# An attention stage of one 128-token tile, with and without an identity matmul per item whose result nobody reads

## The reference

```python
def one_block(args):
    q_i, k_i, v_i, m_i = args
    s_loc = jnp.where(m_i, jnp.einsum('bqkgd,bskd->bkgqs', q_i, k_i).astype(jnp.float32), NEG_INF)
    s_ctx = jnp.einsum('bqkgd,blkd->bkgql', q_i, k_ctx).astype(jnp.float32)
    p = jax.nn.softmax(jnp.concatenate([s_loc, s_ctx, sink_col], axis=-1), axis=-1).astype(v.dtype)
    return (jnp.einsum('bkgqs,bskd->bqkgd', p[..., :n_loc], v_i)
            + jnp.einsum('bkgql,blkd->bqkgd', p[..., n_loc:n_loc + L], v_ctx))
```

## Time and profile before

| | |
|---|---|
| median of three runs | 3007.74 us (3006.69 to 3013.98) |
| the profiled execution's own time | 3018.25 us |
| its span, first to last instruction | 3015.9 us |
| mean granted clock of TensorE over the span | 0.815 of full speed |
| PE busy | 2077.2 us, 69% of the span |
| DVE busy | 1703.2 us, 56% |
| POOL busy | 1703.4 us, 56% |

### The profile page before, as it was taken

How to read it: one execution, slowest core, us unless ns; L and a number is a source line. 1 busy time by engine, 2 the same in 40 slices (tenths; PEclk the granted TensorE clock), 3 DMA queues, 4 the chain that set the end, 5 groups by cost and what they waited for, 6 DMA issues and landing times.

```text
span 3015.9 us, 23744 instructions
## 1 busy us (share of the span) xinstructions
PE 2077.2 (69%) x7806; PEld 908.8 (30%) x7806; DVE 1703.2 (56%) x4169; ACT 371.9 (12%) x753; POOL 1703.4 (56%) x1541
## 2 busy tenths in 40 slices
PE   6998857778886885566566565567968766555555
PEld 2445542224542541111112111113755333111111
DVE  1224496657876686454545664523479677566551
ACT  1111111002211110010011100101212111000000
POOL 0000035766666767777876776760025776777775
PEclk9997978888888897887787776688885998667789
DMA  6462377999899999999999999994167999999998
GB/s 196 156 199 77 98 244 282 406 392 377 320 344 364 359 374 391 399 398 398 398 402 355 349 379 346 367 342 149 40 225 240 370 384 391 372 369 391 388 409 309
DMA packets 339769, 961.00 MB, mean 319 GB/s; under 512 B 27952, under 2 KB 112064, under 8 KB 339264
## 3 DMA queue, kind: packets, MB, share of 16 engines
q0 software_dynamic: 221184, 805.40, 70.4%
q1 hardware_dynamic: 114448, 146.60, 14.3%
q10 hardware_dynamic: 4016, 7.49, 0.7%
HBM read 958.33 MB, written 1.05 MB: 318 GB/s over the span
## 4 chain that ended last, share of the span: by engine, by line
POOL 31%; PE 28%; DMA 15%; DVE 13%; issue 12%; ACT 1%; SPq 0%; POOLq 0%; ACTq 0%; DVEq 0%
POOL v_rows L401 16%; POOL u_rows L401 15%; DMA v_rows<-in_peer_v,idx_turned 12%; PE ps L504 7%; PE ps L704 6%; PE ps L439 3%; DVE u_rows L1341 3%; PE ps L635 2%; PE ps L673 2%; PE ps L429 1%; PE ps L575 1%; DMA u_rows<-in_peer_u,idx 1%; PE ps L466 1%; PE ps L554 1%; PE ps L553 1%
## 5 line engine op out<-in xcount | busy, mean ns | idle before, releaser
L704 PE MATMUL ps<-v_rows,spread_w 128*32 128x512 f32 x3072 | 958.9, 778 | 743.1 <-DMA v_rows<-in_peer_v,idx_turned 714.3
L401 POOL DMA_INDIRECT u_rows<-in_peer_u,idx x768 | 857.2, 1116 | 982.4 <-DVE idx L1284 556.7
L1341 DVE CUSTOM_DVE_ANT_0 u_rows<-u_rows,h 128x1024 f32<-128x1024 f32 x768 | 924.5, 1223 | 570.2 <-DMA u_rows<-in_peer_u,idx 567.7
L401 POOL DMA_INDIRECT v_rows<-in_peer_v,idx_turned x768 | 844.2, 1099 | 315.5 <-issue 221.1
L704 PEld LDWEIGHTS ps<-v_rows,spread_w 128*32 128x32 f32 x3072 | 193.9, 127 | 1369.7 <-issue 1331.8
L504 PE MATMUL ps<-wring,arena 128*128 128x512 f32 x576 | 268.5, 623 | 9.3 <-DVE arena L1002 7.2
L439 PE MATMUL ps<-wring,silu_c 128*2 128x256 f32 x768 | 203.1, 426 | 10.2 <-DMA wring<-in_mod_w 10.2
L673 PE MATMUL ps<-arena,wring 128*128 128x256 f32 (+1 forms) x1024 | 190.6, 342 | 2.8 <-ACT h L870 2.8
L673 PEld LDWEIGHTS ps<-arena,wring 128*128 128x128 f32 x1024 | 163.0, 201 | 47.6 <-issue 28.7
L504 PEld LDWEIGHTS ps<-wring,arena 128*128 128x128 f32 x576 | 113.6, 202 | 163.8 <-issue 150.5
L429 PE MATMUL ps<-table,arena 128*128 128x128 f32 (+1 forms) x480 | 89.9, 317 | 51.6 <-ACT arena L753 32.9
(11 more groups left out here) (159 smaller groups left out, 1737.0 us busy)
## 6 DMA issues: line engine op xcount, KB each, us to landing
wring<-in_mod_w SPq DMA_DIRECT2D x48, 1024.0 KB, 15.7
wring<-in_peer_w_q SPq DMA_DIRECT2D x32, 1024.0 KB, 9.6
wring<-in_ab_w_in SPq DMA_DIRECT2D x28, 1024.0 KB, 5.3
wring<-in_swa_w_in SPq DMA_DIRECT2D x14, 1024.0 KB, 10.8
u_rows<-in_peer_u,idx POOLq DMA_INDIRECT x768, 6.6
v_rows<-in_peer_v,idx_turned POOLq DMA_INDIRECT x768, 6.6
wring<-in_ab_w_out SPq DMA_DIRECT2D x8, 1024.0 KB, 6.4
wring<-in_swa_w_out SPq DMA_DIRECT2D x8, 1024.0 KB, 7.4
```

The source lines that it names most:

```text
L401: nc.gpsimd.indirect_dma_start(out=ring[:, n, :], out_offset=None, in_=table, in_offset=bass.IndirectOffsetOnAxis(ap=index, axis=0)).then_ ...
L704: mm = nc.tensor.matmul(PS[32 * q:32 * q + 32, 6 + e, :], spread_w[:, s // PAIR % 2, 32 * c:32 * c + 32], VB[:, x % NV, e * 512:(e + 1) * ...
L1341: nc.vector.tensor_tensor_reduce(UB[:, slot % NU, :], UB[:, slot % NU, :], H2[:, g // 8 % 3, :], 1.0, 0.0, ALU.mult, ALU.add, av_[:, 0, g ...
```

## The change

`keep_busy` and its call are taken out. Nothing else differs, on any engine; all 18 matmuls of it go, and no semaphore, wait or buffer changes.

```diff
@@ -515,12 +515,6 @@
                         mm.then_inc(pr_tr, 1)
                     yield
 
-            def keep_busy(p):
-
-
-                if p == 2:
-                    nc.tensor.matmul(PS[:, 6, 0:TOK], ident, TB[:, T_MASK:T_MASK + TOK], start=True, stop=True)
-
             def attn(p):
                 i0, i1 = I_OF[p]
                 j = [0, 1, 4, 4][p]
@@ -554,7 +548,6 @@
                             nc.tensor.matmul(PS[:, i % 2, 0:TOK], q, k[:, 0:TOK], start=False, stop=True)
                             mm = nc.tensor.matmul(PS[:, i % 2, TOK:2 * TOK], q, k[:, TOK:2 * TOK], start=True, stop=True)
                         mm.then_inc(at_s, 1)
-                    keep_busy(p)
                     if i0 <= i - 1 < i1:
                         m = i - 1
                         pe.wait_ge(at_exp, m + 1)
```

## The result

The changed kernel takes 3033.87 us (median of 7 runs, 3026.69 to 3039.25); the kernel before, in the runs beside it, 3007.74 us (3000.13 to 3019.04, 7 runs). The ratio is 1.0074, with a 95% interval of 1.0043 to 1.0104. The profiled execution of the changed kernel took 3031.06 us, its span is 3029.3 us. Of all executions behind this document one was slow, one of the ten of fill_keep (7280.29 us), and it is not counted.

What follows compares the result with a forecast made beforehand. PE alone was taken to bound the pass 2 attention; staying at 1.2 GHz gave +17.2 us to L466 and +2.0 in `outp(2)`, together +19.2: 3037.4 from the profiled time, 3026.9 from the median. It took 3034, range 3011 to 3043.

Steps and rivals of the forecast that it cites:

- PE is the bound, without and with L522: Pass 2 attention: PE alone holds the path at both clocks; 1.9 us of slack at full clock, 1.35 without L522.
- The clock stays low through pass 2: Pass 2 attention without L522 stays at 1.2 GHz throughout, items 5.61 us as in pass 3; forecast case 67%.
- The removal of 18 L522: Pass 2 items: each identity matmul removed saves 1.01 us at low clock, 0.54 at full; six ran low, twelve full.
- The stage: Pass 2 attention at 1.2 GHz throughout: L466 starts at 2188.5 instead of 2171.29, +17.2 us.
- The wait for the first exponentials: Start of the attention: second item's scores would end before the first exponentials, losing 0.35 to 0.4 of 2.0 us.
- The row broadcast and transposes of `outp(2)`: After the attention: they start at half clock, which rises 4 to 4.9 us later; +2.0 us, bounds 1.4 and 3.
- Profiled time or median: Whole kernel: +19.2 us added to the profiled 3018.25 gives 3037.4, to the median 3026.9; 3034 taken, nearer the first.
- The first rival: Pass 2 attention: the clock rises anyway without L522; 3009.9 or 2999.3 us, 2996.4 if within 5 us; 13%.
- The second: Pass 2 attention: the clock rises by chance late, in item 8 say; 3019, between 3010 and 3030 us; 12%.

Runs made afterwards that it cites:

- fill_keep: fill with L522 kept in every iteration; 3054.42 us (median of nine), ratio 0.9996 to the kernel before.
- fill_tight: fill with one more 256-column matmul in each of three remaining waits and before item 0's transposes; 2991.27 us, ratio 0.9916 to the kernel before.
- before_again: The kernel before, unedited, profiled once more; stage 64.5 us, full clock after 15.6 us.
- the third session: One of three follow-up sessions on different chips; the kernel before had a median of 3013.79 us in it.
- after_third: The changed kernel unedited, a third time, with timed runs; median 3035.86 against 3013.79 us for the kernel before, ratio 1.0075.
- half_own: The kernel before with L522 on 64 rows, the same half as the item's scores; 3044 to 3051 us, ratio 1.0096 to the kernel before.
- fill: The changed kernel plus unread 512-column identity matmuls where PE waits, none in the items; 3042.37 against 3055.44 us for the kernel before, ratio 0.9963.
- first_items: The kernel before with L522 as two 512-column matmuls in the first three iterations only; 3044.39 against 3055.44 us, ratio 0.9977.
- after_again: The changed kernel, unedited, once more for one profile; stage 91.0 us, its one run 3088.13 us.

## Why the prediction was right

It gave 3034 us, slower; 3033.87 was measured. By its steps:

- **PE is the bound, without and with L522.** Right. In the changed kernel PE is busy for 90.0 of 90.9 us, and no full item has a gap.
- **The clock stays low through pass 2.** Right: 0.50 from first to last full item in three profiles of three. The stretch of pass 3 in the trace of before was the same loop and foretold the item of 5.61 us exactly.
- **The removal of 18 L522.** The cost of one at the low clock was set at 0.95 to 1.01 us. The items differ by 6.57 - 5.61 = 0.96. At full clock 0.54 was read between two starts; the whole items differ by 3.45 - 2.97 = 0.48. The transposes behind take 0.43 us to the next start with L522 (before) and 0.50 without it (fill_tight), so the distance of two starts overstated L522 by about a tenth:

```profile
2138.39 0.60 PE L429 MATMUL ps<-table,arena 128*128 128x128 f32 x4
2138.82 1.00 PE L575 MATMUL ps<-arena 128*128 128x64 f32 x8
```
```profile
2112.58 0.66 PE L429 MATMUL ps<-table,arena 128*128 128x128 f32 x4
2113.08 1.00 PE L579 MATMUL ps<-arena 128*128 128x64 f32 x8
```

- **The stage.** +17.2 us expected to L466, +17.1 measured. The wait for the first exponentials that was foreseen (0.35 to 0.4 us) is there, with 0.18 us idle before L429 at 2093.84; those transposes began 6.55 us after the first score matmul, where 6.6 was expected.
- **The row broadcast and transposes of `outp(2)`.** +2.0 us expected. They ran almost wholly at 0.50, and full clock came 5.7 us after the start of L466, somewhat later than the 4 to 4.9 of the estimate. From L466 to the transposes it is 3.58 us instead of 1.89, from there to the projection 2.62 instead of 2.16 (the wait for ACT before L628 is 0.4 us shorter). Together +2.15.
- **Profiled time or median.** This was the weak step. The 10.5 us between the profiled execution and the median were put down to a late rise in pass 2, and 3034 was taken between 3027 and 3037. A late rise does happen: before_again is 9.4 us shorter in that stage. But in the first pair of profiles the attention of before also began 10.1 us later than that of after, by the stages in front, and that alone is as large. So 3034 was a value between two cases whose cause was guessed, and that it met the median within 0.2 us is luck; the range is what the reasoning carried. What the runs support is the difference: 26 us of medians here, 22 in the third session, against 19.3 and 28.7 to the start of the projection in the two pairs of profiles.

The first rival, in which the clock rises anyway, did not come in any of three profiles. The second, a rise late in the attention, came nearest in after_third, in the drain. The first one's price was near what a high clock gives: with the clock up from the start, the stage without L522 is 51.1 us, and the sum, which began at the low clock, had 2149.4 - 2097.4 = 52.0. So taking L522 out is right once the clock is up, and wrong while it is what brings the clock up.

The Trainium skill, in "TensorE: Matmul & The Clock Gate", part 1, ties full clock to some microseconds of sustained matmul activity. The dense starts of the earlier trace rows agree, with full clock after 4 to 4.9 us. The attention does not: 90 us of PE with hardly a gap stayed at 0.50, and so did 106 us with 64-row L522 in half_own. The part on oscillation on the same page, by which gaps in PE's work throttle it again, agrees: the fall came in the waits of the last projection or right behind them, 5.3 to 8.4 us before the attention, and did not come in fill and fill_tight, where they were filled. In fill_keep, where they were filled too, it came 1.3 us into the attention.

## What to carry to other kernels

Before an instruction of no use is taken out, look at the granted clock around it, and for the same loop elsewhere in the trace without it: pass 3 answered the question before any run. A matmul that only keeps TensorE busy is paid in every item when it stands inside the loop; put where PE waits for another engine, it delayed nothing here, and in two profiles of three held the clock at 2.4 GHz from the start (51 us for the stage instead of 64 to 74). And read a change of 20 us in its stage: the total of one execution moved by 10 us for other reasons.

## What the hardware showed that was not expected

In these profiles the clock held on work on which it did not rise. The items without L522 held 1.00 for 12 to 16 items in first_items, fill and fill_tight, and ran 13 or more items at 0.50 without reaching 1.00 in after, after_again and after_third.

Two 64-row matmuls on different halves of the array ran at the same time, 0.02 us apart, and the second one overtook an instruction ahead of it; in those items L522 cost nothing (5.61 us with it and without). The Trainium skill says in "TensorEngine Tiling (Array Packing)", under key properties, that such tiles operate independently; the trace agrees. The score products here come in just this form, and heads of odd and even number could be paired so; that was not tried.
